# Neighbourhood attention over two or three of four key tiles, with tokens in column order

## The reference, cut to what matters

```python
kh = min(NA_KH_MAX, rows)                       # 8: all rows
row_start = jnp.clip(ri - kh // 2, 0, rows - kh)      # always 0
col_start = jnp.clip(ci - kw // 2, 0, GRID_W - kw)    # kw = 16
col_ok = (ci[None, :] >= col_start[:, None]) & (ci[None, :] < col_start[:, None] + kw)
bias = rpb.astype(F32)[:, dr[:, None, :, None], dc[None, :, None, :]]
sc = jnp.einsum('bijhe,biawhe->bhijaw', qg, kr).astype(F32) * (e ** -0.5) + bias[None]
sc = jnp.where(col_ok[:, None, :], sc, NEG_INF)
```

## Time and profile before

| | us |
|---|---|
| median of 3 runs | 1914.32 (1913.36 to 1916.51) |
| profiled execution | 1913.42 |
| its span | 1911.5 |
| PE busy | 1616.8 (85%) |
| DVE busy | 618.6 (32%) |
| ACT busy | 445.7 (23%) |
| POOL busy | 209.6 (11%) |

### The profile page before, as it was taken

One profiled execution on the slowest core, in us unless ns is written; L12 is line 12 of the kernel. 1 busy time (PEld: TensorE's weight loads), 2 busy tenths in 40 slices (PEclk: granted clock), 3 DMA queues, 4 the chain that ended last, 5 costly groups with the idle time before them and its releaser, 6 DMA issues. The chain is left out here.

```text
span 1911.5 us, 22815 instructions
## 1 busy us (share of the span) xinstructions
PE 1616.8 (85%) x7556; PEld 797.3 (42%) x7556; DVE 618.6 (32%) x1337; ACT 445.7 (23%) x1001; POOL 209.6 (11%) x215
## 2 busy tenths in 40 slices
PE   5999888998887988888779999899688788888873
PEld 2456544453333443333335555455333333333331
DVE  1266365142222122222253825622322222222223
ACT  2110656212111111111121036542111111111111
POOL 2000022110111011111020002101111111111100
PEclk8999999989999999999979999999799989999996
DMA  9522444068999999999872324513399999999993
GB/s 349 167 88 101 163 152 152 12 241 321 411 403 407 352 391 407 406 412 414 348 257 88 110 81 160 196 45 112 133 396 374 404 414 403 408 408 403 394 399 155
DMA packets 119092, 527.50 MB, mean 276 GB/s; under 512 B 17008, under 2 KB 23248, under 8 KB 69872
## 3 DMA queue, kind: packets, MB, share of 16 engines
q1 hardware_dynamic: 101520, 493.66, 66.3%
q0 software_dynamic: 13104, 24.51, 4.1%
q10 hardware_dynamic: 4400, 8.46, 1.2%
HBM read 521.06 MB, written 23.86 MB: 285 GB/s over the span
## 5 line engine op out<-in xcount | busy, mean ns | idle before, releaser
L1205 PE MATMUL ps<-ring,arena 128*64 128x512 f32 x2928 | 702.3, 638 | 158.8 <-DMA ring<-in_w_exp_up 131.6
L1205 PEld LDWEIGHTS ps<-ring,arena 128*64 128x64 f32 x2928 | 255.6, 147 | 561.9 <-issue 557.6
L894 PE MATMUL ps<-ring,hT 128*128 128x512 f32 (+1 forms) x768 | 256.1, 490 | 5.4 <-ACT tmp L1380 4.9
L627 DVE TENSOR_TENSOR arena<-ps,arena 64x512 f32<-64x512 f32 (+1 forms) x64 | 44.4, 693 | 666.3 <-ACT arena L1477 574.6
L894 PEld LDWEIGHTS ps<-ring,hT 128*128 128x128 f32 x768 | 145.5, 192 | 104.0 <-issue 88.6
L1477 ACT ACTIVATE arena<-ps 128x512 f32<-128x512 f32 x64 | 38.2, 597 | 633.7 <-PE ps L1205 582.8
L859 POOL DMA_INDIRECT yexp_d<-arena,masks x64 | 59.2, 925 | 910.5 <-DVE arena L637 910.5
L1469 ACT ACTIVATE arena<-ps,modc 128x128 f32<-128x128 f32 x256 | 96.2, 456 | 261.1 <-PE ps L1190 261.0
L1085 PE MATMUL ps<-ring,hT 128*128 128x512 f32 x256 | 112.5, 595 | 0.0
L635 DVE TENSOR_TENSOR arena<-ps,gate 64x512 f32<-64x512 f32 (+1 forms) x64 | 43.7, 684 | 149.6 <-PE ps L1205 134.8
L1614 DVE SCALAR_TENSOR_TENSOR probsT<-z,convw,probsT 128x512 f32<-128x512 f32 x120 | 90.0, 751 | 3.9
(11 more groups left out here) (200 smaller groups left out, 1322.2 us busy)
## 6 DMA issues: line engine op xcount, KB each, us to landing
ring<-in_w_exp_gate SPq DMA_DIRECT2D x128, 1024.0 KB, 15.2
ring<-in_w_exp_up SPq DMA_DIRECT2D x128, 1024.0 KB, 19.2
ring<-in_w_exp_down SPq DMA_DIRECT2D x128, 1024.0 KB, 12.1
ring<-in_w_ada SPq DMA_DIRECT2D x24, 2048.0 KB, 8.8
ring<-in_w_in SPq DMA_DIRECT2D x8, 2048.0 KB, 20.4
ring<-in_w_out SPq DMA_DIRECT2D x4, 2048.0 KB, 8.1
ring<-in_w_in SPq DMA_DIRECT2D x6, 1024.0 KB, 10.9
xn_d<-arena ACTq DMA_DIRECT2D x8, 512.0 KB, 5.0
```

The costliest lines, as they stand in the source:

```text
L894: last = pe.matmul(out, lhs(k), rhs(k), start=(k == 0), stop=(k == n - 1))
L1205: last = [pe.matmul(outs[c][HALF * c:HALF * c + HALF, :], lhs(k)[:, 0:HALF], rhs(c, k), start=(k == 0), stop=(k == n - 1), tile_position=( ...
```

## The change: column order

Only group B is touched, with the norm of C that stands beside its values.

- Tokens of B are in column order (8 * column + row), so a tile of 128 is 16 whole columns and a query tile needs only key tiles 0 to 1, 0 to 2, 1 to 3 or 2 to 3. Scores, maxima, exponentials, turned probabilities and value products are cut to 256 or 384 keys.
- q and k are still made in token order; the drain of their transposes (`qk_out`) writes them permuted.
- Values: two products of 512 columns (weights stationary, hT streaming through a strided view) give them transposed. ScalarE drains them into the unused half of their own weight slot, and eight transposes turn them back, two to a bank of value tile.
- C's variance products now follow all value products; its Ln and Exp stand ahead of the four value drains.
- `heads_out` writes yT back in token order through the same strided view.
- The bias table is in column order, again 896 columns a head (256 + 384 for two edges and the middle shared), and comes in one DMA a head instead of two; the mask moves from the constants to the tail of the dilation table.

```diff
+COLS_T = P // GRID_H
+KEY_TILES_B = [(0, 2), (0, 3), (1, 4), (2, 4)]
+BIAS_AT = [0, 2 * P, 2 * P, 5 * P]
+BIAS_W = 7 * P
+MASK_W = BIAS_W // GRID_H
+def key_tiles(u):
+    return KEY_TILES_B[UNITS[u][2]] if UNITS[u][0] == "B" else (0, TT)
+def key_count(u):
+    return P * (key_tiles(u)[1] - key_tiles(u)[0])
...
+            if g == "B":
+                for f in range(2):
+                    take((l, "vT", f), "mm")
+                for f in range(2):
+                    take((l, "var", f), "mm")
             for t in range(TT):
                 take((l, "v", g, t), "mm")
-                if g == "B" and t == 1:
-                    for f in range(2):
-                        take((l, "var", f), "mm")
...
+        def by_columns(buf, row, first, width, tokens):
+            return view(buf, row * S + first, [[KD * S, P], [1, width], [GRID_W, tokens]])
+        def values_turned(l, f):
+            return slot(UNIT["win", l, 2 + 2 * GROUPS.index("B")])[:, 2 * f:2 * f + 2, GW:2 * GW]
...
-                        for up in range(2):
-                            n = rows_b * GRID_W
-                            pool.dma_start(bias_t[hp][GRID_W * up:GRID_W * up + GRID_W, n * h:n * h + n],
...
+                        pool.dma_start(bias_t[hp][:, BIAS_W * h:BIAS_W * h + BIAS_W], a["rpb"][l, 2 * hp + h]).then_inc(bias_in, 16)
...
-                        cm = view(cst, C_AT["colmask"], [[NCONST, P], [0, rows_b], [1, GRID_W]])
+                        tab = bias_t[hp][:, BIAS_W * h:BIAS_W * h + BIAS_W].rearrange("p (w r) -> p w r", r=GRID_H)
+                        cm = view(masks, 2 * S - P, [[2 * S, P], [1, MASK_W], [0, GRID_H]])
...
+                    if g == "B":
+                        for f in range(2):
+                            key = (l, "vT", f)
+                            await_free(pe, key)
+                            fills(product(bank(key), lambda k: slot(unit)[:, k, P * f:P * f + P],
+                                          lambda k: by_columns(hT, k, 0, GRID_W, GRID_H)), key)
+                            qk_turn(g, f + 2)
+                        group_norm(1)
+                        for f in range(2):
+                            await_drained(pe, (l, "vT", f))
+                        for t in range(TT):
+                            key = (l, "v", g, t)
+                            await_free(pe, key)
+                            for f in range(2):
+                                last = pe.transpose(bank(key)[:, P * f:P * f + P],
+                                                    values_turned(l, f)[:, t // 2, P * (t % 2):P * (t % 2) + P], ident)
+                            fills(last, key)
+                        continue
...
-                        fills(pe.matmul(bank(key), qkT[g][p0:p0 + n, hp, P * t:P * t + P], qkT[g][p0:p0 + n, 2 + hp, :],
-                                        start=True, stop=True, tile_position=(p0, 0)), key)
+                        k0, k1 = key_tiles(u)
+                        fills(pe.matmul(bank(key)[:, 0:P * (k1 - k0)], qkT[g][p0:p0 + n, hp, P * t:P * t + P],
+                                        qkT[g][p0:p0 + n, 2 + hp, P * k0:P * k1], start=True, stop=True, tile_position=(p0, 0)), key)
...
-                        for kt in range(TT):
+                        for kt in range(key_count(u) // P):
                             last = pe.transpose(bank4(key)[:, kt, :], src[:, P * kt:P * kt + P], ident)
...
-                    for kt in range(TT):
+                    k0, k1 = key_tiles(u)
+                    for kt in range(k0, k1):
...
+                        dst, src = qkT[g][:, :, P * t:P * t + P], bank4(key)
+                        if g == "B":
+                            rows = P // GRID_W
+                            dst = qkT[g].rearrange("p f (c r) -> p f r c", r=GRID_H)[:, :, rows * t:rows * t + rows, :]
+                            src = src.rearrange("p f (r c) -> p f r c", c=GRID_W)
...
+                    if g == "B":
+                        for f in range(2):
+                            key = (l, "vT", f)
+                            await_filled(act, key)
+                            drains(act.activation(values_turned(l, f), bank(key).rearrange("p (a n) -> p a n", a=2), ACT.Copy), key)
+                            qk_out(f + 2)
+                        for f in range(2):
+                            key = (l, "var", f)
+                            await_filled(act, key)
+                            drains(act.activation(tmp[:, f, :], bank(key), ACT.Ln, bias=C["eps"]), key)
+                        for f in range(2):
+                            await_drained(act, (l, "var", f))
+                            act.activation(tmp[:, f, :], tmp[:, f, :], ACT.Exp, scale=-0.5).then_inc(log_ready, 1)
...
+                            dst = dst[:, 0:key_count(u)]
+                            act.activation(dst, dst, ACT.Exp, scale=-1.0, bias=negm[:, n:n + 1],
...
-                            first = (RPB_H - 1) * GRID_W * h + (GRID_H - 2 - 2 * t) * GRID_W
-                            table = bias_t[hp][:, first:first + S]
+                            first = BIAS_W * h + BIAS_AT[t]
+                            table = bias_t[hp][:, first:first + key_count(u)]
...
+                    if g == "B":
+                        y = by_columns(yT, FIRST_F[g] + hp, COLS_T * t, COLS_T, GRID_H)
+                        heads, sums_inv = (r.rearrange("p (c r) -> p c r", r=GRID_H) for r in (heads, sums_inv))
+                    drains(dve.tensor_tensor(y, heads, sums_inv, ALU.mult), key)
```

More of the change, by code:

```diff
@@ L1063, in attend @@
                         await_drained(pe, (l, "v", g, TT - 1))
[L1064 removed]
+                    k0, k1 = key_tiles(u)
+                    for kt in range(k0, k1):
                         for h in range(2):
                             c0 = HD * (2 * hp + h)
[L1067 to L1068 removed]
+                            last = pe.matmul(bank(key)[HD * h:HD * h + HD, 0:P], v[g][:, kt, c0:c0 + HD], probT[2 * (j % 2) + h][:, kt - k0, :],
+                                             start=(kt == k0), stop=(kt == k1 - 1), tile_position=(0, HD * h))
                     fills(last, key)
@@ L1373, in _ @@
                         drains(act.activation(v[g][:, t, :], bank(key)[:, 0:GW], ACT.Copy), key)
-                        if t < 2:
+                        if t < 2 and g != "B":
                             qk_out(t + 2)
[L1376 to L1380, removed]
-                            for f in range(2):
-                                await_drained(act, (l, "var", f))
-                                act.activation(tmp[:, f, :], tmp[:, f, :], ACT.Exp, scale=-0.5).then_inc(log_ready, 1)
                 for f in range(2):
@@ L1413, in prob_out @@
                             act.wait_ge(conv_ready, 2 * (l + 1))
-                        dst = probT[2 * (j % 2) + (head if g == "A" else h)]
-                        drains(act.activation(dst, bank4(key), ACT.Copy), key)
+                        dst, nk = probT[2 * (j % 2) + (head if g == "A" else h)], key_count(u) // P
+                        drains(act.activation(dst[:, 0:nk, :], bank4(key)[:, 0:nk, :], ACT.Copy), key)
                 def rinv_out(u):
@@ L1711, in maxima @@
                         else:
-                            first = (RPB_H - 1) * GRID_W * h + (GRID_H - 2 - 2 * t) * GRID_W
-                            table = bias_t[hp][:, first:first + S]
+                            first = BIAS_W * h + BIAS_AT[t]
+                            table = bias_t[hp][:, first:first + key_count(u)]
                         await_filled(dve, key)
-                        drains(dve.tensor_tensor_reduce(unit_probs(u)[h][:, :], bank(key), table, -HD ** -0.5, 3.0e38, ALU.add, ALU.min,
+                        keys = slice(0, key_count(u))
+                        drains(dve.tensor_tensor_reduce(unit_probs(u)[h][:, keys], bank(key)[:, keys], table, -HD ** -0.5, 3.0e38, ALU.add, ALU.min,
                                                         negm[:, n:n + 1]), key)
@@ L1740, in heads_out @@
                     dve.wait_ge(rT_ready, NPAIR * l + j + 1)
-                    drains(dve.tensor_tensor(yT[:, FIRST_F[g] + hp, P * t:P * t + P], bank(key)[:, 0:P], rT[:, j % 2, :], ALU.mult), key)
+                    y, heads, sums_inv = yT[:, FIRST_F[g] + hp, P * t:P * t + P], bank(key)[:, 0:P], rT[:, j % 2, :]
+                    if g == "B":
+                        y = by_columns(yT, FIRST_F[g] + hp, COLS_T * t, COLS_T, GRID_H)
+                        heads, sums_inv = (r.rearrange("p (c r) -> p c r", r=GRID_H) for r in (heads, sums_inv))
+                    drains(dve.tensor_tensor(y, heads, sums_inv, ALU.mult), key)
                 def squares_a():
@@ L1850, in shape_constants @@
             out[name + g] = tab.reshape(TT, P, w).transpose(1, 0, 2).reshape(P, TT * w)
-    col = np.arange(GRID_W)
-    start = np.clip(col - NA_W // 2, 0, GRID_W - NA_W)
```

(15 more changed lines are left out.)

25 lines of the change are left out of this document (10 added, 15 removed).

## The result

| | kernel before | changed kernel |
|---|---|---|
| median (6 runs each) | 1914.17 us (1913.36 to 1916.51) | 1926.61 us (1922.04 to 1930.47) |
| profiled execution, its span | 1913.42, 1911.5 | 1925.41, 1923.6 |
| PE, DVE, ACT, POOL busy | 1616.8, 618.6, 445.7, 209.6 | 1633.8, 614.4, 441.1, 202.8 |

The ratio is 1.0065 [1.0049, 1.0081]. The forecast was 1904.3 and its range ended at 1920; what came is rival (a), the slow strided stream.

A forecast was written before the change was run, and what follows sets the result against it. Expert stages were taken as bound by loads, mixers by TensorE and the engines it trades with. 2.9 - 7.9 = -5.0 a layer, -10.0 in all, gives 1903.4 profiled, median 1904.3; range 1897 to 1920.

The forecast's parts named there:

- rival (a): B's turned value products: the strided stream takes 0.86 us a record, +16.6 us in all, 1931; chance 13%.
- What bounds the kernel: Whole kernel: expert stages bound by their loads, the edited mixers by TensorE and the engines it trades with.
- what the mixer saves moves everything: Behind the mixers: savings there move all later work forward, since expert loads wait for ring slots that TensorE frees.
- 0.5 us a layer for the stride: B's value products: streaming hT at a step of 64 elements costs 4%; upper bound +13.8 us a layer.
- The 5%: Two rows of transposes, strided against plain stationary operand: 7 loads in 0.84 us against 0.80, the nearest rows for the stride.
- The rule that the prediction cites: Trainium skill on SBUF: reads within one 16-byte line run at full bandwidth, each access crossing to a new line pays; no price.
- the norm's order, +2.4: Value stage: C's norm behind all value products delays ScalarE's free time and D's first scores; stage +2.9 a layer with the stride.
- Part 2: B's maps: fewer key tiles save 7.9 us a layer (first pair 3.3, second pair and behind it 4.6); bounds -4.5 to -9.5.
- pure steps: B's map steps with no ada or mod product beside them: held by the return loop, they save only 0.3 to 0.4 us.
- Rival (b): B's maps: the loop through DVE and ScalarE keeps steps from shrinking, -4.5 a layer; 1912, no difference; chance 16%.
- Part 3: Bias table, mask and permuted writes: hidden, 0; bounds 0 to +2.5 for bias and mask, 0 to +1 a layer for writes.
- Rival (c): Gap ahead of D's first scores: half clock over five us costs 2.5 to 3 us a layer, 1909 to 1910; chance 11%.

The follow-up runs named there:

- experiment 1: Changed kernel, but B's value products stream hT plainly in token order and the drain of the turned values permutes instead: 1902.25 us, ratio 0.9933.
- Experiment 2: Kernel before, with C's input products streaming hT at various steps and the stationary operands of A's and B's value products strided: one execution, 1947.95 beside 1927.49.
- experiment 3: experiment 1 with C's variance products moved between B's two turned value products: 1891.20 us, ratio 0.9874; its repeat 1891.83, ratio 0.9860.
- experiment 5: experiment 3 with all three permuted writes (q and k, turned values, heads) made plain, so the output is wrong and only stretches count: 1906.54 us.

## Why the prediction was wrong, by its own steps

- **What bounds the kernel.** Right in that the mixers carried the loss. But the prediction named expert stages of another length as the sign that "what the mixer saves moves everything" is wrong, and they were 5.1 and 1.5 us shorter. The sum had no term for the clock in stretches that nobody edits.
- **Part 1, "0.5 us a layer for the stride".** This is the step that failed. Measured: 0.437 us a record more, 32 records, 14.0 a layer, 28.0 in all (experiment 1, the other way round: 13.4 a layer). The upper bound (+13.8) and rival (a) had both mechanism and size; the weight between them was wrong. The 5% came from weight loads of transposes. They read 128 columns, a quarter of the stream, and I now take their spacing to be set by the transposes beside them and not by how fast the operand is read, which no run shows. Experiment 2 shows how little such rows can tell: at step 4 the same price that doubles a stream adds 0.02 us a record when it falls on the stationary operand. A row in which the disputed access is hidden behind something else bounds nothing. The rule that the prediction cites had no row of a stream against it, and I gave it 13%.
- **Part 1, the norm's order, +2.4.** Right in kind: ScalarE's two table loads, Ln and Exp stand between TensorE and the first scores. Beyond the slower stream it is 3.0 in the changed kernel (17.0 - 14.0) and 3.5 in layer 0 of experiment 1, whose drain of the turned values is permuted as well; experiment 3 takes 3.4 to 3.6 of it away. The +2.4 was counted to ScalarE's free time; to D's first scores, the mark used here, the prediction's own times give 212.1 - 208.7 = 3.4, of which 2.9 without the stride, so this step was right in size too.
- **Part 2, -7.9 a layer.** 7.2 measured. First pair -2.95 (forecast -3.3), second -3.14 (-3.9), the two last units -1.1 (-0.7). The steps' own estimate was off in both directions: pure steps of the second pair fell from 3.33 to 2.25 and 2.53 us (0.8 to 1.1, where 0.3 to 0.4 was forecast), but the change-over kept 2.57 of its 3.21 us of waiting for heads out, and new waits of 0.89 and 0.48 for the same came in. Rival (b) did not happen.
- **Part 3, nothing.** Right for bias and mask: the mask operation took 1.74 us instead of 2.08, no longer, and the second pair's table was ready at 329.02, 3.0 us ahead of the maxima that need it. The permuted writes were not free: 0.7 us a layer in experiment 5, within the bound of 1. That is for experiment 3's form, which permutes the drain of the turned values too; in the changed kernel that drain is plain (0.60 us), so its own price is not measured.
- **Rival (c), the clock.** The drop came, its price didn't. In both executions of the changed kernel and in experiment 1, in both layers, the granted clock was 0.50 for the first 3.1 to 6.2 us from D's first scores, behind a stretch in which TensorE mostly waited for ScalarE; the kernel before has no drop at that place, nor has experiment 3 in layer 0. (c) asked 2.5 to 3 us a layer for it. From D's first scores to those of its ninth unit it is 29.68 us in experiment 3 without a drop, 29.69 to 29.72 in the changed kernel with 3 us of half clock behind the mark, and 30.45 with 6: nothing, or 0.8. The kernel before, without a drop, takes 30.31. Other stretches at half clock, of 3.4 to 13.7 us, come and go in all kernels, in B's maps and in the units of D and A; one of 3.4 us made the maps 1.4 us longer (33.86 and 32.46 in experiment 3 and its repeat).
- **The range.** Its lower end is miscounted: -9.5 + 2.4, doubled, is -14.2, which gives 1900 and not 1897. The miss is at the other end.
- **The sum.** With 13.5 a layer beyond the 0.5 counted for the stride, the forecast of the span becomes 1911.5 - 10.0 + 27 = 1928.5; measured 1923.6. Router and experts are 6.7 shorter (5.1 and 1.5), everything else together 1.8 longer. Without the stride the forecast is 1904.3 - 1 = 1903.3, and experiment 1, nearly that kernel, gave 1902.3. That this agrees so well is partly luck: its profiled span is 18.6 below the kernel before, and only half of that comes from the mixers, the other half from the stretches that nobody edited. The sign was decided by one term all the same: without its 27 us the loss of 12 is a gain.

## What to carry to other kernels

When an operand's view changes, look at how many neighbours of each 16 bytes it reads in a row, not at how far it jumps: choose the order of the data so that pairs stay together, and a transposing stream costs next to nothing (7.15 us for 16 records here against 14.03). Put a permutation where its cost is hidden or small, and a serial piece on another engine (table loads, Ln, Exp) beside a product, not behind the last one. And price an unseen access only from a row in which that access sets the pace; if there is none, a bound is all you have, and the two ends deserve nearly equal weight.

## What the runs showed of the hardware that I had not expected

- A float32 stream of 512 columns takes 0.43 to 0.45 us a record when contiguous, at a step of 2 or in pairs at a step of 64, and 0.86 to 0.92 at steps of 4, 8, 16 and 64; the same step on the 128 columns of a stationary operand adds 0.024 us.
- Writes of the other engines went the same way. A drain of 512 elements on ScalarE, written at a step of 8, took 1.10 us, in pairs 0.66 (as two instructions of 256), plain 0.60. VectorE's heads, 128 elements, took 0.38 permuted and 0.29 in pairs or plain. Other steps were not tried.
- A stretch at half clock costs what stands behind it. On a product followed by a wait for weights it cost nothing that could be seen; on one followed by work that was ready, 16.96 us were measured instead of 13.97. The wait for weights itself made no difference: after 4.60 us of it or 2.20, that product started 16.7 or 16.8 us behind the expert before.
